# One 512-column matmul in place of two 256-column ones in the four output projections

## The chip, the cores and the metric

The kernel runs on one core of one Trainium2 chip. The metric is the device time of one execution in microseconds (us). Single matmuls are told in nanoseconds (ns).

## What is computed

Two small networks follow each other on one sequence of 256 tokens with a model width of 2048, all in 32-bit floats. Cut to what the change touches:

```
# first block: state-space mixer, then sparse attention, each with a residual and a layer norm
proj = x @ w_in;  yg = gated, scan-mixed rows of width 4096
h = yg @ ssd_w_out                      # 4096 -> 2048   (o1)
x = layer_norm(ALPHA * x + h)
o = attention rows of width 4096, gated
h = o @ dsa_w_out                       # 4096 -> 2048   (o2)
x = layer_norm(ALPHA * x + h)
# second block: gated MLP, then stick-breaking attention, each with a residual
y = u * mixed * silu(zg)                # width 4096
h = h + y @ a_w_out_2                   # 4096 -> 2048   (o3)
o = attention rows of width 2048, gated
h = h + o @ b_w_out_2                   # 2048 -> 2048   (o4)
return rms_norm(h, final_g)
```

## The kernel before

Every weight matrix is streamed once from memory. A unit is one stretch of 1024 columns' worth of weights: SyncE fetches it in 512 KB into one of four `RAW` buffers, ScalarE rounds it to a high part (`wh`, line 1074), VectorE forms the low part (`wl`, line 1502), both in the TensorE type float32r, and TensorE multiplies three times: activations high by weights high, high by low, low by high. `Plan` sets the order of the units and the buffers into which they go, and TensorE, ScalarE, VectorE and SyncE all walk that order; small tasks of other steps (transposes, attention products) run between two units.

In most projections the weights are the stationary operand and 256 tokens are the moving one, so that a matmul has 256 columns. In the projections that are in `TOKENS` it is the other way round: 128 tokens of the activation tile `X` are stationary and the weights move. Those are the four output projections `o1` to `o4`, and `cq`, `v5` and `v7`. The three last stream up to 512 columns of weights in one matmul; the output projections stream 256 at a time (line 750).

An output projection is cut into five blocks of columns, `LAST_COLS`: three of 512 columns and two of 256. For each 128 rows of the contraction there are two token halves `t` and three products, and in a block of 512 columns each of these is two matmuls, at columns 0 and 256, with the same stationary tile, which is loaded anew for each. A 512-column unit has two such 128-row tiles: 2 x 2 x 3 x 2 = 24 matmuls. A 256-column unit has four tiles and 24 matmuls also. A block of 512 float columns fills one PSUM bank of `G` for each token half.

Where a buffer starts within 512 bytes is set by hand: `STILL` is byte 128 and `MOVING` is byte 496. The activations of the output projections, `YY`, start at `STILL`. Their weights lie in the buffers `W0m`, `W1m` and `W2m` and, for some units, in spare buffers `WA`, `WB` and `WC`; all these start at `MOVING`. Most other projections use `W0` to `W2`, `WY` and `W7`, at `STILL`, with the activations `AA` and `CQ` at `MOVING`. `cq` and the first units of `v5` and `v7` have `AA` stationary; from there on `v5` and `v7` use a copy of it in the upper half of `YY`, which the profile names `YY`. All tiles are multiples of 512 bytes apart from these starts. The profile prints one line number, 672, for all matmuls, since a helper `mm` issues them; 685 is the helper for transposes.

Of the kernel before, what the change touches and what calls it, by code (L numbers as in the profile page):

```python
# [194 lines left out]
def program(nc, A, out, at, bank, counting):  # L195
# [38 lines left out]
    def on(*event):  # L234
        if counting:
            return unit_done.sem, 1
        name, n = at[event]
        return signals[name].sem, n
# [428 lines left out]
    def tensor_program():  # L667
# [3 lines left out]
        def mm(o, l, r, start, stop):  # L671
            return e.matmul(o, l, r, start=start, stop=stop, skip_group_check=True)  # L672
# [16 lines left out]
        def unit(u, part=None):  # L689
            b, kts, width, _ = units[u]  # L690
            name, i = b
# [44 lines left out]
            for j, k in enumerate(kts):  # L736
                if u == 0 and j == 1:
                    e.wait_ge(*on("rest", 0))
                if name == "bc" and i == 0 and k % 2 == 0:
                    e.wait_ge(*on("xt", k))  # L740
                if name in ("q", "qi") and i == 0 and k == 0:
                    e.wait_ge(*on("cq"))
                if name in ("o1", "o2", "o3", "o4") and i < 2 and k % 4 == 0:
                    e.wait_ge(*on(name + "_in", k // 4))
                if b in (("cq", 0), ("v5", 0)) and k % 4 == 0:
                    e.wait_ge(*on("at1" if name == "cq" else "at2", k // 4, 1 if part is None else part))
                if b == ("q7", 0) and P * k in [c for c, _ in LAST_COLS]:
                    e.wait_ge(*on("at3", k))
                if name in TOKENS:
                    step = 256 if name in ("o1", "o2", "o3", "o4") else 512  # L750
                    cols = range(0, width, step)
                    for t in range(2) if part is None else (part,):
                        xh, xl = (X[:, k, q, t * P:(t + 1) * P] for q in range(2))
                        for x, w in ((xh, wh), (xh, wl), (xl, wh)):
                            for c in cols:
                                last = mm(G[:, half + t, c:c + min(step, width)], x, w[:, j, c:c + min(step, width)],
                                          k == 0 and c == 0 and x is xh and w is wh, k == nk - 1 and x is xl)
                else:
                    for f in range(width // P):
                        o = G[:, half + f // 2, (f % 2) * T:(f % 2 + 1) * T]  # L760
                        h, l = wh[:, j, f * P:(f + 1) * P], wl[:, j, f * P:(f + 1) * P]
                        mm(o, h, X[:, k, 0, :], k == 0 and f % 2 == 0, False)
                        mm(o, h, X[:, k, 1, :], False, False)
                        last = mm(o, l, X[:, k, 0, :], False, k == nk - 1)
# [266 lines left out]
        def set8():  # L1031
            here(unit_done, "end7", "unit")
            here(pe_made, "end7", "pe")
            yield

        walk(unit, dict(turn_in=turn_in, dt_task=dt_task, ssd=ssd, gate_z=gate_z, ln_close=ln_close,
                        set3=set3, ev_cq=ev_cq, ev_ms=ev_ms, index=index, attend=attend,
                        set4=set4, ev_u5=ev_u5, set6=set6, ev_o3=ev_o3, scale7=scale7,
# [1353 lines left out]
```

## Time and profile before

| what | value |
|---|---|
| median of three runs | 2424.24 us (2424.21 to 2425.11) |
| span of the profiled execution | 2422.2 us |
| what lies outside the span (median less span) | 2.0 us |
| TensorE busy in the span | 2412.6 us of 2422.2, 19584 matmuls |
| VectorE, ScalarE busy | 1571.3 us (65%), 1243.8 us (51%) |
| weights and data moved | 467.90 MB, mean 193 GB/s |

The duration of one matmul in the profile (275 ns for 256 columns) holds its way through the array, which overlaps with the next one. What a stream of matmuls costs is read from their starts: the start of the group behind less the start of the group, divided by the count.

### The profile page before, as it was taken

Reading aid. Unit: us, or ns where it says so; the run is one execution under the profiler, and the core shown is the slowest. Engines: PE = TensorE matmul, PEld = TensorE weight load, DVE = VectorE, ACT = ScalarE, POOL = GpSimd, SP = SyncE. Lnnn points to the kernel's source line nnn. Section 1 sums busy time; section 2 is a strip of 40 time slices with the busy share of each in tenths; the row PEclk is TensorE's granted clock in tenths of the full one; section 3 lists DMA queues with packets and bytes.
Section 4 is the critical chain, followed back from the end, with each engine's and each line's share of the span. In section 5 each row is a group of like instructions: output and inputs, shape, how many; then the busy total and the mean of one; then the engine's idle time right before and its main releaser. Section 6 shows DMA issues by size and latency. Waiting matters only on the chain.

```text
span 2422.2 us, 45365 instructions
## 1 busy us (share of the span) xinstructions
PE 2412.6 (100%) x19584; PEld 2336.7 (96%) x19584; DVE 1571.3 (65%) x2104; ACT 1243.8 (51%) x1427; POOL 88.8 (4%) x68
## 2 busy tenths in 40 slices
PE   9999999999999999999999999999999999999998
PEld 9999999999999999999988899999999999999998
DVE  6778888865577766665575556656655555555556
ACT  5446665654364565554464445445444445455463
POOL 0001000100031000000000000000000000000002
PEclk9999999999999999999999999999999999999999
DMA  8666666657755655547657666666655576655645
GB/s 258 197 194 185 207 189 186 187 182 246 235 164 165 192 166 149 161 152 243 222 193 240 196 198 194 194 185 196 182 188 190 188 239 204 184 173 173 192 157 183
DMA packets 265048, 467.90 MB, mean 193 GB/s; under 512 B 18512, under 2 KB 68240, under 8 KB 262928
## 3 DMA queue, kind: packets, MB, share of 16 engines
q1 hardware_dynamic: 264704, 464.74, 61.9%
q8 instruction: 154, 2.52, 0.4%
q14 instruction: 46, 0.38, 0.0%
q10 hardware_dynamic: 144, 0.26, 0.0%
HBM read 452.16 MB, written 4.26 MB: 188 GB/s over the span
## 4 chain that ended last, share of the span: by engine, by line
PE 98%; DVE 1%; DMA 1%; ACT 0%; issue 0%; ACTq 0%
PE G L672 91%; PE M L672 5%; PE M L685 1%; DMA RAW<-in_ssd_w_in 1%; DVE W2m L1502 0%; DVE W0m L1502 0%; DVE E L1585 0%; ACT W0m L1074 0%; DVE E L1626 0%; DVE SZ L1656 0%; DVE E L1587 0%; DVE W L1498 0%; ACT L1154 0%; DVE W L1502 0%; DVE W1m L1502 0%
## 5 line engine op out<-in xcount | busy, mean ns | idle before, releaser
L672 PE MATMUL G<-AA,W 128*128 128x256 f32 x7908 | 936.7, 277 | 0.6 <-DVE AA L1506 0.4
L672 PEld LDWEIGHTS G<-AA,W 128*128 128x128 f32 x7908 | 914.7, 188 | 5.6 <-issue 3.5
L1502 DVE TENSOR_TENSOR W<-RAW,W 128x1024 fp32r<-128x1024 f32 (+1 forms) x445 | 556.0, 1252 | 361.1 <-ACT W L1074 359.9
L1074 ACT CAST W<-RAW 128x1024 fp32r<-128x1024 f32 (+1 forms) x445 | 463.7, 1047 | 457.1 <-PE G L672 447.7
L672 PE MATMUL G<-AA,WY 128*128 128x256 f32 x2508 | 304.2, 277 | 0.0
L672 PEld LDWEIGHTS G<-AA,WY 128*128 128x128 f32 x2508 | 293.0, 188 | 1.7 <-issue 1.2
L1502 DVE TENSOR_TENSOR WY<-RAW,WY 128x1024 fp32r<-128x1024 f32 (+1 forms) x112 | 140.9, 1260 | 73.8 <-ACT WY L1074 73.8
L672 PE MATMUL G<-W0m,YY 128*128 128x256 f32 x1512 | 183.7, 276 | 0.4 <-DVE W0m L1502 0.2
L672 PE MATMUL G<-W1m,YY 128*128 128x256 f32 x1512 | 183.1, 276 | 0.1
L672 PE MATMUL G<-W,YY 128*128 128x512 f32 x792 | 181.3, 389 | 0.0
L672 PE MATMUL G<-W2m,YY 128*128 128x256 f32 x1488 | 180.4, 276 | 0.0
L672 PEld LDWEIGHTS G<-W,YY 128*128 128x128 f32 x792 | 148.4, 188 | 30.7
L672 PEld LDWEIGHTS G<-W0m,YY 128*128 128x128 f32 x1512 | 176.9, 188 | 1.0 <-DVE W0m L1502 0.8
L672 PEld LDWEIGHTS G<-W1m,YY 128*128 128x128 f32 x1512 | 176.6, 188 | 0.8 <-DVE W1m L1502 0.6
L672 PEld LDWEIGHTS G<-W2m,YY 128*128 128x128 f32 x1488 | 174.0, 188 | 0.2
L1074 ACT CAST WY<-RAW 128x1024 fp32r<-128x1024 f32 (+1 forms) x112 | 116.2, 1043 | 100.2 <-PE G L672 98.6
L1502 DVE TENSOR_TENSOR W1m<-RAW,W1m 128x1024 fp32r<-128x1024 f32 x63 | 78.5, 1246 | 77.0 <-ACT W1m L1074 76.9
L1502 DVE TENSOR_TENSOR W2m<-RAW,W2m 128x1024 fp32r<-128x1024 f32 x62 | 76.9, 1240 | 68.9 <-ACT W2m L1074 68.6
L1502 DVE TENSOR_TENSOR W0m<-RAW,W0m 128x1024 fp32r<-128x1024 f32 x63 | 78.2, 1241 | 65.3 <-ACT W0m L1074 65.1
L1074 ACT CAST W1m<-RAW 128x1024 fp32r<-128x1024 f32 x63 | 66.2, 1050 | 82.6 <-PE G L672 78.7
L1074 ACT CAST W0m<-RAW 128x1024 fp32r<-128x1024 f32 x63 | 66.2, 1051 | 80.9 <-PE G L672 80.8
L1074 ACT CAST W2m<-RAW 128x1024 fp32r<-128x1024 f32 x62 | 65.2, 1052 | 80.2 <-PE G L672 78.5
(301 smaller groups left out, 2387.4 us busy)
## 6 DMA issues: line engine op xcount, KB each, us to landing
RAW<-in_a_w_in SPq DMA_DIRECT2D x192, 512.0 KB, 4.0
RAW<-in_ssd_w_in SPq DMA_DIRECT2D x160, 512.0 KB, 4.4
RAW<-in_b_w_in SPq DMA_DIRECT2D x128, 512.0 KB, 4.0
RAW<-in_dsa_w_in SPq DMA_DIRECT2D x72, 512.0 KB, 3.6
RAW<-in_ssd_w_out SPq DMA_DIRECT2D x64, 512.0 KB, 4.8
RAW<-in_dsa_w_out SPq DMA_DIRECT2D x64, 512.0 KB, 4.1
RAW<-in_a_w_out SPq DMA_DIRECT2D x64, 512.0 KB, 3.7
RAW<-in_b_w_out SPq DMA_DIRECT2D x32, 512.0 KB, 3.7
```

What stands on the lines that cost most here:

```text
L672: return e.matmul(o, l, r, start=start, stop=stop, skip_group_check=True)
L685: return e.transpose(o, i, idn)
L1074: e.copy(wh[:, 0:n], RAW[:, v % NR, 0:n]).then_inc(*up(cast_done, "cast", v))
L1502: e.tensor_tensor(wl[:, 0:n], RAW[:, v % NR, 0:n], wh[:, 0:n].bitcast(F), ALU.subtract).then_inc(*up(rest_done, "rest", v))
```

## The change

In the projections of `TOKENS` the step over the weight columns becomes 512 for all, so that `o1` to `o4` stream a 512-column tile in one matmul. Blocks of 256 columns keep one matmul of 256 for each product. Buffers and their addresses, the order of the units, the products and their order within a tile, the signals and everything on the other engines stay.

```
                 if name in TOKENS:
-                    step = 256 if name in ("o1", "o2", "o3", "o4") else 512
+                    step = 512
                     cols = range(0, width, step)
```

TensorE's instructions at the start of `o1`, among the last tasks of the state-space mixer, before:

```order
L672 MATMUL G<-W0m,YY 128x256 x24
L685 MATMUL M<-ident,XG 128x128 x4
L672 MATMUL G<-W2m,YY 128x256 x24
L685 MATMUL M<-ident,XG 128x128 x4
L672 MATMUL G<-W1m,YY 128x256 x24
```

and now:

```order
L672 MATMUL G<-W0m,YY 128x512 x12
L685 MATMUL M<-ident,XG 128x128 x4
L672 MATMUL G<-W2m,YY 128x512 x12
L685 MATMUL M<-ident,XG 128x128 x4
L672 MATMUL G<-W1m,YY 128x512 x12
```

Nothing moved: 24 matmuls of a unit became 12 of twice the width, and the transposes stand between the same units.

TensorE's instructions near the end of `o4`, where the last 512-column block ends and the first of 256 columns begins, before:

```order
L672 MATMUL G<-W0m,YY 128x256 x24
L672 MATMUL G<-W2m,YY 128x256 x24
L672 MATMUL G<-W1m,YY 128x256 x24
L672 MATMUL G<-W0m,YY 128x256 x24
L672 MATMUL G<-W2m,YY 128x256 x24
```

and now:

```order
L672 MATMUL G<-W0m,YY 128x512 x12
L672 MATMUL G<-W2m,YY 128x512 x12
L672 MATMUL G<-W1m,YY 128x256 x24
L672 MATMUL G<-W0m,YY 128x256 x24
L672 MATMUL G<-W2m,YY 128x256 x24
```

The last three rows, units of a 256-column block, are the same in both.

## Rows read from the trace of the kernel before

**Rows 1.** The page's head: busy us (share of span) x instructions; then clock by slice.

```profile
span 2422.2 us, 45365 instructions
PE 2412.6 (100%) x19584; PEld 2336.7 (96%) x19584; DVE 1571.3 (65%) x2104; ACT 1243.8 (51%) x1427; POOL 88.8 (4%) x68
...
PEclk9999999999999999999999999999999999999999
```

**Rows 2.** The page's chain that ended last, by engine and by line.

```profile
PE 98%; DVE 1%; DMA 1%; ACT 0%; issue 0%; ACTq 0%
PE G L672 91%; PE M L672 5%; PE M L685 1%; DMA RAW<-in_ssd_w_in 1%; DVE W2m L1502 0%; DVE W0m L1502 0%; DVE E L1585 0%; ACT W0m L1074 0%; DVE E L1626 0%; DVE SZ L1656 0%; DVE E L1587 0%; DVE W L1498 0%; ACT L1154 0%; DVE W L1502 0%; DVE W1m
```

**Rows 3.** Waits of TensorE: waiting line, releaser, us in total, times, longest.

```profile
PE M L672 <- POOL ident L2265: 1.6, 1, 1.6
PE G L672 <- DVE AA L1506: 0.4, 2, 0.3
PE G L672 <- DVE W0m L1502: 0.2, 1, 0.2
PE G L672 <- DVE W L1502: 0.2, 1, 0.2
```

**Rows 4.** Groups by line and shape: count, busy us, mean ns, idle before.

```profile
L672 PE MATMUL G<-W0m,YY 128*128 128x256 f32 x1512 | 183.7, 276 | 0.4 <-DVE W0m L1502 0.2
L672 PE MATMUL G<-W1m,YY 128*128 128x256 f32 x1512 | 183.1, 276 | 0.1
L672 PE MATMUL G<-W2m,YY 128*128 128x256 f32 x1488 | 180.4, 276 | 0.0
...
L672 PE MATMUL G<-WB,YY 128*128 128x256 f32 x408 | 47.7, 275 | 0.0
L672 PE MATMUL G<-WA,YY 128*128 128x256 f32 x408 | 47.6, 275 | 0.0
...
L672 PE MATMUL G<-WC,YY 128*128 128x256 f32 x48 | 5.9, 275 | 0.0
```

**Rows 5.** Timeline (start us, length us) of TensorE inside o1.

```profile
640.77 2.88 PE L672 MATMUL G<-W1m,YY 128*128 128x256 f32 x24
643.49 2.88 PE L672 MATMUL G<-W0m,YY 128*128 128x256 f32 x24
646.21 13.76 PE L672 MATMUL G<-WA,YY 128*128 128x256 f32 x120
659.81 1.52 PE L672 MATMUL G<-W2m,YY 128*128 128x256 f32 x12
```

**Rows 6.** Timeline of TensorE: v5 from the copy in YY, then u5.

```profile
1296.29 109.00 PE L672 MATMUL G<-W,YY 128*128 128x512 f32 x480
1405.13 8.36 PE L672 MATMUL G<-AA,W 128*128 128x256 f32 x72
```

**Rows 7.** Timeline of TensorE: cq, with AA stationary.

```profile
685.39 8.56 PE L672 MATMUL G<-W,AA 128*128 128x512 f32 x36
693.79 2.94 PE L672 MATMUL G<-WA,AA 128*128 128x512 f32 x12
696.57 0.64 PE L672 MATMUL G<-AA,W 128*128 128x256 f32 x4
```

**Rows 8.** Timeline of TensorE: 384-column products of the stick-breaking attention.

```profile
2031.00 0.33 PE L672 MATMUL M<-SPH,TGR 128*128 128x384 f32 x1
2031.17 0.34 PE L672 MATMUL M<-SPL,TGR 128*128 128x384 f32 x1
```

**Rows 9.** Page's groups: weight loads, us busy, mean ns, idle before.

```profile
L672 PEld LDWEIGHTS G<-W,YY 128*128 128x128 f32 x792 | 148.4, 188 | 30.7
L672 PEld LDWEIGHTS G<-W0m,YY 128*128 128x128 f32 x1512 | 176.9, 188 | 1.0 <-DVE W0m L1502 0.8
```

**Rows 10.** Timeline of TensorE: a unit right behind transposes, o3 and v5.

```profile
1815.79 1.04 PE L685 MATMUL M<-ident,RES 128*128 128x128 f32 x8
1816.58 3.04 PE L672 MATMUL G<-W2m,YY 128*128 128x256 f32 x24
1819.46 2.88 PE L672 MATMUL G<-W1m,YY 128*128 128x256 f32 x24
...
1226.97 3.04 PE L672 MATMUL G<-WB,AA 128*128 128x512 f32 x12
1229.85 0.60 PE L685 MATMUL M<-ident,XH 128*128 128x128 f32 x4
```

**Rows 11.** Busy us by engine in stretches of o1, o3; then clock, DMA share, GB/s.

```profile
575.00:620.00 45.00, 45.00 (x399) 45.00 (x399) 28.47 (x28) 20.42 (x20) 0.00 (x0) 1.00 0.78 254
...
1820.00:1860.00 40.00, 40.00 (x355) 40.00 (x354) 21.07 (x22) 16.35 (x18) 0.00 (x0) 1.00 0.57 193
```

## The prediction, made before the changed kernel ran

> **What bounds the kernel now.** I read the head of the page first: the reader is to see that TensorE is busy for 2412.6 of 2422.2 us and that its granted clock stands in the top tenth in all 40 slices [rows 1]. The chain that ended last confirms it: 98% TensorE, 91% of it products into G [rows 2]. Last the waits: in the whole execution TensorE waits for other engines 2.4 us, and 0.2 us of it is in an output projection [rows 3]. So the time is the sum of the distances between the starts of 19584 matmuls, and the question is whether two starts of 256 columns take longer than one of 512. What the other engines do counts only if TensorE gets ahead of them.
>
> **How many matmuls the change touches.** The three 512-column blocks of an output projection take 2 token halves x 3 products x 3 blocks x 2 column halves = 36 matmuls for each 128 rows of the contraction. There are 32 + 32 + 32 + 16 = 112 such row tiles in the four projections, so 4032 matmuls of 256 columns become 2016 of 512, and 2016 weight loads fall away with them. The two 256-column blocks have 2 x 3 x 2 x 112 = 1344, which stay. Together 5376, and the groups with YY stationary and 256 columns hold 1512 + 1512 + 1488 + 408 + 408 + 48 = 5376 [rows 4]. In us: 4032 at the rate read below are 457 us, 19% of the span, and 1 ns on each merged matmul is 2.0 us.
>
> **The rate now.** In o1, 120 matmuls from WA start at 646.21 and the next group at 659.81: 13.60 us / 120 = 113.33 ns each. The units on both sides have 24 in 2.72 us, the same 113.3 [rows 5]. Two of them, which is what one new matmul replaces, take 226.67 ns. At 2.4 GHz, the upper of the clock's two levels and the one granted there (1.00) [rows 11], 256 columns are 106.67 ns and 512 are 213.33, so there is an overhead of 6.67 ns on a matmul of 256. The whole question is whether this overhead belongs to the matmul or to its columns.
>
> **The rate then, from the nearest rows.** The kernel has 512-column matmuls with the stationary tile in the same buffer YY, at the same start within 512 bytes: v5, once it reads its copy. 480 of them run from 1296.29 to 1405.13: 108.84 us / 480 = 226.75 ns [rows 6]. That is twice 113.33 within 0.1 ns: the overhead went with the columns. What differs from the changed kernel is one thing, the start of the moving weights: byte 128 there, byte 496 in W0m, W1m, W2m, WA, WB and WC. In cq, where AA at byte 496 is stationary, the start of the moving weights can be compared: 36 matmuls from W (byte 128) take 8.40 us, 233.3 ns each, and 12 from WA (byte 496) take 2.78 us, 231.7 ns each [rows 7]. The start of the moving side makes little difference there, and the stationary side's makes 6.6 ns (233.3 against 226.75). Stationary at 128 and moving at 496 with 512 columns does not occur in the trace. I take 226.75, the row with the same stationary buffer and more than an order of magnitude more matmuls. The steady part is 2016 x (226.75 - 226.67) = +0.2 us. The bounds on both sides: above, the 233.3 of cq, 2016 x 6.67 = +13.4 us; below, the bare 213.33 ns of the columns, 2016 x 13.33 = -26.9 us, which no stream of this type in the trace reaches.
>
> **Breaks.** At 18 places in the 512-column blocks tasks of other steps stand between two units. The unit behind such a break takes longer: in o3 2.88 us from start to start against 2.72, so +0.16 [rows 10]. The 512-column unit behind transposes in v5 also takes 2.88, which is +0.16 over twelve at 226.67 and +0.08 over twelve at its own 233.3 [rows 10]. So each break costs the same as now or 0.08 less: 0 to -1.4 us, and I take -0.4, nearer to none, since the stationary side of that row is the other one. The signal of a unit comes with its last matmul, which starts 113 ns earlier than now and is 114 ns longer (389 mean against 275), so that VectorE and ScalarE see each unit end at the same time as before.
>
> **Other work.** Nothing is added elsewhere. VectorE and ScalarE are busy for 28.47 and 20.42 of 45 us in a stretch of o1, 21.07 and 16.35 of 40 in o3, and the DMA queues 0.78 and 0.57 [rows 11]: if the units became 3% shorter (2.64 us), these would stand at some 65%, 47% and 0.80, and still deliver. This cover is needed only in the faster case. At the start of o1 VectorE is late once already, by 0.2 us [rows 3]; a faster unit would wait there, at most some tenths of a us.
>
> **Sum.** Against the profiled execution: 2422.2 + 0.2 - 0.4 = 2422.0 us span; with the 2.0 us that lie outside, 2424.0 us. A measurement of this kernel tells about 0.2%, 4.8 us, from no change, which is 2.4 ns on each merged matmul.
>
> **Rival 1: the overhead is one for each matmul, faster.** For: every matmul loads its stationary tile, the loader's groups in the 256-column stream are busy nearly without idle (176.9 us busy, 1.0 idle), and with 512 columns it has 30.7 us of idle on 148.4 busy [rows 9], so the 256-column rate could be the loader's. Then 512 at byte 496 would pay the 6.67 ns once: 220.0 ns, 2016 x 6.67 = -13.4 us, 2410.6. The one row with a moving side at byte 496 and a stationary side at 128 that is wider than 256 is the 384-column product: 170 ns from start to start [rows 8]. In proportion to columns it would be 170.0 and with one overhead 166.67; the row is read to 10 ns only and decides nothing by itself. A path between, the 170 and 128 bare columns (53.3), gives 223.3 ns, -6.8 us, 2417.2. Against: 226.75 in v5 [rows 6], where a matmul also has one load and pays 13.4 ns. The rival must hold that byte 128 on the moving side costs that second 6.7 ns.
>
> The Trainium skill has a rule of this kind ("TensorE: Matmul & The Clock Gate", Back-to-back issue gap): N / 2.4 + 2.5 ns for each matmul when the clock is up, a fixed part that a merged matmul pays once. By it the change would give 2016 x 2.5 = 5.0 us, 2419. This trace does not agree: the rule has 109.2 and 215.8 ns where the rows have 113.33 and 226.75 [rows 5, 6]. The same section has sustained streams at other rates, which no row here shows either.
>
> **Rival 2: the long stream at byte 496 does not fall into step with the loads, slower.** The rate of 512-column matmuls depends on where operands start: 226.75, 231.7, 233.3 [rows 6, 7]. The 256-column stream at 128/496 has the good rate, and so has the 512-column one at 128/128; nothing says that 512 at 128/496 has it. If each merged matmul behaves as those of cq do, the place is every unit of the 512-column blocks and the price is 2016 x (231.7 - 226.67) = +10.1 us to 2016 x 6.67 = +13.4 us: 2434.1 to 2437.5. It decides against me from 2.4 ns on each. Against: in cq the slow rate stays whichever start the moving side has, so it goes with the stationary side.
>
> **Rival 3: nothing of it happens.** The instruction order of the changed kernel shows twelve 128x512 where there were twenty-four 128x256, in all 512-column blocks, so this is excluded.
>
> **How the numbers follow.** Forecast (in proportion to columns, 2422.6 to 2425.5): 0.42. Rival 1 in its two sizes, 2410.6 to 2417.2, and the rule of the Trainium skill beside it: 0.30. Rival 2, 2434 to 2437.5: 0.28. Faster by over 0.2% (under 2419.4) takes rival 1, 0.31; slower by over 0.2% (over 2429.1) takes rival 2, 0.28; within, 0.41. Both signs hold more than the forecast, so its own range stands apart: 2422.6 to 2425.5. The range for 8 in 10 reaches over both rivals: 2409.5 to 2438.0. It leaves out a rate under 219.5 ns and one over 233.5.
>
> **What would show it.** In the changed kernel the timeline of o1 between 575 and 626 us is a stream without breaks: a unit of twelve takes 2.72 us if I am right, 2.64 for the single overhead, 2.78 to 2.80 for rival 2. v5's 480 matmuls must still take 108.84 us, and the 256-column blocks 2.72 a unit. TensorE's waits must stay at 2.4 us. If the units take 2.72 and the time still differs, the cause is the breaks or the waits. I would be wrong first in the step that takes v5's rate for a moving side that starts elsewhere.

## The result and the profile after

| | median | runs |
|---|---|---|
| before | 2424.23 us (2423.46 to 2426.29) | 8 |
| changed | 2430.66 us (2430.08 to 2431.54) | 8 |

The ratio is 1.0027, with a 95% interval of 1.0018 to 1.0036: the change makes the kernel slower by 0.27%, 6.4 us. The forecast was no change at 2424.0; the time lies inside the wide range and outside the forecast's own.

The head of the page after, with the same columns as [rows 1]:

```profile
span 2429.7 us, 41333 instructions
...
PE 2419.7 (100%) x17568; PEld 2255.5 (93%) x17568; DVE 1571.8 (65%) x2104; ACT 1243.3 (51%) x1427; POOL 88.4 (4%) x68
...
PEclk9999999999999999999999999999999999999999
```

19584 - 2016 = 17568 matmuls, as foretold; 2016 weight loads are gone; VectorE and ScalarE work as before; the clock is at its upper level throughout. TensorE is busy 7.1 us longer all the same. The timeline of TensorE (start us, length us) in o1 shows where:

```profile
609.77 2.93 PE L672 MATMUL G<-W0m,YY 128*128 128x512 f32 x12
612.55 8.48 PE L672 MATMUL G<-WA,YY 128*128 128x512 f32 x36
620.87 2.94 PE L672 MATMUL G<-W2m,YY 128*128 128x512 f32 x12
623.64 2.94 PE L672 MATMUL G<-W1m,YY 128*128 128x512 f32 x12
```

A unit of twelve takes 2.77 us from start to start, and 36 matmuls take 8.32: 231.1 ns each, where two of 256 columns took 226.67 [rows 5]. The 480 matmuls of v5 still take 226.75 and the 256-column blocks 113.3, so only the merged ones changed. The single starts in the trace, which the timeline merges, show more: 225, 231, 237 or 238 ns, over and over. Three of them are 693.3, 231.1 on the mean. Before, single starts were 113 or 114 ns apart without any such cycle.

The rate is not the same everywhere. This is o4 in the same execution, around the last task with 128-column products:

```profile
2345.72 2.93 PE L672 MATMUL G<-W2m,YY 128*128 128x512 f32 x12
2348.49 2.93 PE L672 MATMUL G<-W1m,YY 128*128 128x512 f32 x12
...
2352.36 2.94 PE L672 MATMUL G<-W0m,YY 128*128 128x512 f32 x12
2355.14 2.88 PE L672 MATMUL G<-W2m,YY 128*128 128x512 f32 x12
2357.86 2.88 PE L672 MATMUL G<-W1m,YY 128*128 128x512 f32 x12
2360.58 1.47 PE L672 MATMUL M<-LSB,V 128*128 128x256 f32 x8
```

Ahead of the task a unit takes 2.77 us, behind it 2.72, from the same buffers. At the start of o1 two short pieces run at 226.7 as well, 48 matmuls from 499.85 and 12 from 513.21, each begun behind a wait.

TensorE's waits after (columns as in [rows 3]):

```profile
PE M L672 <- POOL ident L2265: 1.6, 1, 1.6
PE G L672 <- DVE W1m L1502: 0.7, 1, 0.7
PE G L672 <- DVE AA L1506: 0.4, 1, 0.4
PE G L672 <- DVE W0m L1502: 0.4, 2, 0.3
```

VectorE is 1.1 us late at the start of o1, against 0.2.

**Where the 7.5 us between the two spans lie**, taken between points of equal work in the two traces (the end of a wide block is set 18 matmuls into the 256-column block behind it, so that its settling is counted in): up to o1 -0.7; the first 13 us of o1, with its waits, +0.7; the rest of o1's wide blocks +2.0; o2's +2.2; o3's +2.5; o4's +0.8; everything else -0.1. The head of the kernel, which the change does not touch, took between 0.7 less and 0.1 more than before in the seven kernels below that leave it as it is, so it shifts by some tenths on its own. In a steady stretch of o1, 225 merged matmuls (51.0 us before) take 1.00 us more, 4.4 ns each; o3's 576 take 2.49, 4.3 each.

### The profile page after: what moved, and what is told of

It is laid out like the page before. It is cut to its first block, busy times and chain, and to the rows that moved or that the text cites. A ratio compares the mean times of both kernels' runs of the same rounds, so it can differ in the third digit from the quotient of the medians.

```text
span 2429.7 us, 41333 instructions
## 1 busy us (share of the span) xinstructions
PE 2419.7 (100%) x17568; PEld 2255.5 (93%) x17568; DVE 1571.8 (65%) x2104; ACT 1243.3 (51%) x1427; POOL 88.4 (4%) x68
## 4 chain that ended last, share of the span: by engine, by line
PE 95%; DVE 2%; ACT 1%; DMA 1%; issue 1%; POOL 0%; SPq 0%; ACTq 0%; POOLq 0%
PE G L672 89%; PE M L672 5%; PE M L685 1%; DMA CSB<-cs_scratch 1%; DVE W L1502 0%; ACT W L1074 0%; DVE E L1626 0%; POOL YT L2282 0%; DVE WY L1502 0%; DVE E L1585 0%; DVE XG L1524 0%; DVE E L1587 0%; DVE YT L1640 0%; DVE XG L1531 0%; DVE W1m L1502 0%
## 5 line engine op out<-in xcount | busy, mean ns | idle before, releaser
L672 PE MATMUL G<-W1m,YY 128*128 128x512 f32 (+1 forms) x900 | 185.5, 356 | 0.7 <-DVE W1m L1502 0.7
L672 PE MATMUL G<-W0m,YY 128*128 128x512 f32 (+1 forms) x888 | 185.8, 359 | 0.4 <-DVE W0m L1502 0.4
L672 PE MATMUL G<-W2m,YY 128*128 128x512 f32 (+1 forms) x876 | 182.7, 358 | 0.0
L672 PEld LDWEIGHTS G<-W1m,YY 128*128 128x128 f32 x900 | 148.3, 188 | 27.4 <-DVE W1m L1502 1.3
L672 PEld LDWEIGHTS G<-W0m,YY 128*128 128x128 f32 x888 | 147.5, 188 | 27.7 <-DVE W0m L1502 1.4
L672 PEld LDWEIGHTS G<-W2m,YY 128*128 128x128 f32 x876 | 145.4, 188 | 26.5 <-DVE W2m L1502 0.2
```

## The experiments

Two theories stood at the outset. **A**: where the moving tile starts within 512 bytes decides, together with the width, at what rate a stream settles, and 496 is bad for 512 columns. **B**: the width and the work beside the output projections decide, and the start does not.

**512 columns with the weights at byte 128**, against the changed kernel.

```
-            w = (W3M if units[u][0][0] in ("o1", "o2", "o3", "o4") else W3)[s]
+            w = W3[s]
...
-            o += (MOVING - o) % 512      # in spare(): WA, WB, WC
+            o += (STILL - o) % 512
```

> The changed kernel (512 columns) with the output projections' weights in buffers that start at byte 128 within 512 in place of 496. Theory A (the start of the moving side sets the rate of a 512-column stream): units of twelve take 2.72 us as in v5 (226.7 ns each) and not 2.77 (231.1), so 2016 x 4.4 ns = 8.9 us less than the changed kernel; about 2424 us, as before the change. Theory B (the rate comes from the width and from what runs beside the output projections, the start does not matter): units stay at 2.77 us, time near 2430.7. The spare buffers WA and WB also serve cq and v5 on AA, 120 matmuls, where the start moved the rate by 1.6 ns at most, 0.2 us.

Measured: 2432.3 us, ratio to the kernel before 1.0033 (1.0020 to 1.0045). The total fits B; the timeline does not:

```profile
611.17 8.32 PE L672 MATMUL G<-WA,YY 128*128 128x512 f32 x36
619.33 8.32 PE L672 MATMUL G<-W,YY 128*128 128x512 f32 x36
627.49 11.68 PE L672 MATMUL G<-WA,YY 128*128 128x256 f32 x96
639.00 6.16 PE L672 MATMUL G<-W,YY 128*128 128x256 f32 x50
```

36 of 512 columns take 8.16 us: 226.7 ns, as A has it; between points of equal work the wide blocks take what they took before, within 0.1 us each, beyond the first 13 us of o1 (+1.0). But the 256-column blocks, whose buffers had moved too, take 11.51 us / 96 = 119.9 ns and not 113.3. There are 1344 of these, 9.0 us by count and 8.6 found, and they give back what the wide ones had gained. The expectation had counted one width alone.

**256 columns with the weights at byte 128**, the same edit on the kernel before.

> The kernel before (256 columns in the output projections) with their weights at byte 128. Theory A in its wide form (start and width together decide, and 496 is there for the 256-column stream): 256 columns at 128 are slower than 113.3 ns, with 118 to 120 ns as right behind a break; 5376 matmuls x 5 to 6.7 ns = +27 to +36 us, 2451 to 2460. Theory B: 113.3 ns whatever the start, no change, 2424.2.

Measured: 2457.23 us, ratio 1.0136 (1.0121 to 1.0151), 32.9 us more than the kernel before, measured beside it (2424.38).

```profile
616.51 8.80 PE L672 MATMUL G<-WA,YY 128*128 128x256 f32 x72
625.15 8.80 PE L672 MATMUL G<-W,YY 128*128 128x256 f32 x72
```

8.64 us / 72 = 120.0 ns. B falls: width and neighbours are as before, the start alone turns 113.3 into 120.0. 5376 x 6.67 = 35.8 is about the loss, less the pieces behind breaks that had 118 to 120 before too.

**v5 and v7 with their weights at byte 496**, against the kernel before.

```
-            w = (W3M if units[u][0][0] in ("o1", "o2", "o3", "o4") else W3)[s]
+            w = (W3M if units[u][0][0] in ("o1", "o2", "o3", "o4", "v5", "v7") else W3)[s]
```

> The kernel before, with the weights of v5 and v7 at byte 496 in W0m to W2m in place of 128 (x7's buffer W7 stays). The output projections are as before. Theory A: the 512-column matmuls of v5 and v7 on the copy in YY go from 226.75 to 231.1 ns; 792 matmuls in W buffers, +3.5 us. Theory B: they stay at 226.75.

Measured: 2427.16 us in one run against 2424.38. The stream that the prediction had taken as its nearest row [rows 6], now:

```profile
1310.23 2.93 PE L672 MATMUL G<-W1m,YY 128*128 128x512 f32 x12
1313.00 2.94 PE L672 MATMUL G<-W0m,YY 128*128 128x512 f32 x12
```

2.77 us for twelve: the start alone turns 226.7 into 231.1, in another projection, with the output projections untouched. Between points of equal work the stretch with v5 takes 1.9 us more than before and the one with v7 1.4, 3.2 of the 3.5 expected. Theory A holds both ways.

**A scan of streams alone.** Nothing else runs in this kernel; after four fp32 matmuls each stream begins anew. Its core:

```
for n, so, mo in CASES:                      # columns, start of stationary, start of moving side
    for u in range(8): for j in range(2): for t in range(2):
        for x, w in ((xh, wh), (xh, wl), (xl, wh)):
            for col in range(0, 512, n):
                mm(G[:, t, col:col + n], x, w[:, col:col + n], ...)
    warm(4)
```

> Not the network: 38 streams of 96 (512 columns) or 192 (256) products of the same three-product pattern as in an output projection, one after another behind four fp32 matmuls each, with nothing beside them, over starts of the stationary and the moving side within 512 bytes and over widths. The output is only the input copied. Theory A: with the stationary side at 128, 512 columns take 231.1 ns with the moving side at 496 and 226.7 at 128; 256 take 113.3 at 496; and other starts fall on these or further levels. Theory B: with no other engine at work 512 at 496 takes 226.7 too, and all starts of the moving side are alike. 496/128 and 496/496 should show the 231 to 233 of cq.

The first streams in its timeline are 512 columns at 128/496 (stationary/moving), 512 at 128/128, then 256 at 128/496 and 256 at 128/128:

```profile
23.38 22.43 PE L42 MATMUL G<-W,X 128*128 128x512 f32 x96
45.65 1.05 PE L42 MATMUL M<-ident 128*128 128x128 f32 x8
46.46 22.06 PE L42 MATMUL G<-W,X 128*128 128x512 f32 x96
68.36 1.06 PE L42 MATMUL M<-ident 128*128 128x128 f32 x8
...
115.74 22.07 PE L42 MATMUL G<-W,X 128*128 128x256 f32 x192
137.65 1.05 PE L42 MATMUL M<-ident 128*128 128x128 f32 x8
138.46 23.28 PE L42 MATMUL G<-W,X 128*128 128x256 f32 x192
161.57 1.05 PE L42 MATMUL M<-ident 128*128 128x128 f32 x8
```

From start to start the four take 22.27, 21.90, 21.91 and 23.11 us, the settling included. The distances of starts in the second half of each stream give the settled rate:

| stationary/moving | 512 columns, ns | 256 columns, ns |
|---|---|---|
| 128/496 | 231.1 | 113.3 |
| 128/128 | 226.7 | 120.0 |
| 496/128 | 233.3 | 120.0 |
| 496/496 | 233.3 | 118.3 |
| 0/0, 256/256 | 226.7, 226.6 | 120.0, not run |
| 0/256 | 226.7 | 120.0 |
| 0/368 | not run | 113.3 |

So the loss needs no other engine and no DMA. The scan also shows why cq misled: with the stationary side at 496 both starts of the moving side give 233.3, while at 128 they differ by 4.4.

**A finer scan**: stationary at 128, the moving side at every 16th byte for 512 columns and every 8th for 256.

> Not the network: streams of the three-product pattern alone, stationary side at byte 128, moving side at every 16th byte for 512 columns (72 matmuls each) and every 8th for 256 (144 each). The output is only the input copied. Theory A: each width has its own set of good starts, 512 at 128 and 384 (226.7) and 256 near 496 (113.3), and others lie 2 to 10 ns above per 512 columns. Open: whether any start is under 226.7 or 113.3; if the overhead could be had once for each matmul, some start shows 220 for 512.

Settled at 226.7 with 512 columns: 112, 128, 368 and 384. Settled at 113.3 with 256 columns: 64, 192, 240, 320, 448 and 496. All others lie between 228.8 and 234.7, or 116.6 and 122.5; the values repeat with a period of 256 bytes, within 0.1 ns but for one pair (512 columns at 0 and 256, 1.1 apart). No start of the moving side is good for both widths, and none is under 226.66 or 113.32. The 220 ns of rival 1 does not appear. Not every value repeats at the same addresses: 512 columns at 128/112 ran at 226.7 here and at 236.7 in the first scan, 256 columns at 128/256 at 118.7 here and at 120.0 there, and 512 columns at 128/0 and 128/256 differ by 1.0 between the scans.

**Other products, and another lead.** The rows of the changed kernel at 226.7 and the value at 112 ask whether a stream has one rate at all.

```
made = {"same": ((xh, wh),) * 3, "xonly": ..., "wonly": ...,
        "turned": ((xh, wh), (xl, wh), (xh, wl))}.get(mode, ((xh, wh), (xh, wl), (xl, wh)))
...
if mode[:4] == "lead":                       # two short matmuls of k columns ahead of the stream
    mm(M[:, 0:k], X[:, so:so + P], W[:, mo:mo + k], True, True)   # twice
```

> Not the network: streams at fixed starts with another pattern of products: all three alike (one stationary, one moving tile), only the stationary tile changing, only the moving one, and the second and third product exchanged; then 32 streams of 512 columns at 128/496, each behind two short matmuls of 16 to 512 columns. The output is only the input copied. Theory A1 (the repeating 225, 231, 237 ns is the three products, each with its own distance between tiles): with all products alike a single value stays, with the order exchanged the sequence changes, and what stands ahead does not matter. Theory A2 (it is the phase between two readers that settles into one of two states, 226.7 or 231.1): the lead decides for some of the 32 streams, which run at 226.7 from the start to the end at the same addresses, as three stretches of the changed kernel did.

A1 falls. With all products alike, 512 columns at 128/496 still run 225, 231, 237; the cycle of three has nothing to do with the three products. At 128/128 and 128/384 all five patterns settle at 226.7, and at 256 columns all keep 113.3 (496) and 120.0 (128). At 128/240 four patterns run at 231.1 to 231.3, and the one with all products alike runs at 226.7 from its second matmul on. Whether the products or what stood ahead made that difference, the scan does not tell. A2 stands: of 32 leads at 128/496, those of 64 and 128 columns make the stream run at 226.66 from its second matmul to its last, the other thirty at 230.9 to 231.3. The lead of 64 and its neighbour of 80:

```profile
766.86 0.39 PE L50 MATMUL M<-W,X 128*128 128x64 f32 x2
767.08 16.58 PE L50 MATMUL G<-W,X 128*128 128x512 f32 x72
783.50 1.05 PE L50 MATMUL M<-ident 128*128 128x128 f32 x8
784.31 0.39 PE L50 MATMUL M<-W,X 128*128 128x80 f32 x2
784.53 16.88 PE L50 MATMUL G<-W,X 128*128 128x512 f32 x72
801.25 1.05 PE L50 MATMUL M<-ident 128*128 128x128 f32 x8
```

16.42 against 16.72 us for the same 72 matmuls on the same tiles.

**The start chosen by width**, against the changed kernel.

```
-            w = (W3M if units[u][0][0] in ("o1", "o2", "o3", "o4") else W3)[s]
+            w = (W3M if units[u][0][0] in ("o1", "o2", "o3", "o4") and units[u][2] < 512 else W3)[s]
```

> The changed kernel with the start of W0 to W2 chosen by width in the output projections: byte 128 for units of 512 columns, byte 496 for units of 256 (WA, WB, WC stay at 496). Theory A (each width has its own good start, nothing else was lost): 1848 merged matmuls go from 231.1 to 226.7 ns, -8.1 us against the changed kernel, and the 256-column blocks keep 113.3; 168 from WA and WB stay at 231.1, +0.7 us. So 2423 to 2425, equal to the kernel before. Rival (a part of the loss comes from breaks or waits that 512 columns bring): 1 us or more stays over the kernel before, beyond the 0.7.

Measured: 2424.78 us against 2423.80 of the kernel before, measured beside it, ratio 1.0003 (0.9994 to 1.0013), no difference that the measurement can tell. Between points of equal work, with the 18 matmuls behind, o3's wide blocks take 134.48 us (134.49 before, 136.99 changed). The stretches with WA and WB, still at 496, are 0.5 us longer each, 1.0 and not 0.7, since a stream that changes between the two starts settles anew each time:

```profile
603.32 8.37 PE L672 MATMUL G<-W,YY 128*128 128x512 f32 x36
611.53 8.47 PE L672 MATMUL G<-WA,YY 128*128 128x512 f32 x36
619.84 8.37 PE L672 MATMUL G<-W,YY 128*128 128x512 f32 x36
```

8.21 us for 36 from W right behind WA (228.1 each), 8.31 for WA. TensorE's waits here are near the changed kernel's, 1.4 us for W at line 1502 where that had 1.1 for W1m and W0m. The first 13 us of o1 take 1.1 us more than before and the head of the kernel 0.7 less, where the changed kernel had 0.7 and 0.7: most of the one is given back by the other.

**o3 alone at 512 columns**, against the kernel before.

```
-                    step = 256 if name in ("o1", "o2", "o3", "o4") else 512
+                    step = 256 if name in ("o1", "o2", "o4") else 512
```

> The kernel before with 512-column matmuls in o3 alone, starts as before. Theory A: 576 merged matmuls x 4.4 ns = 2.6 us in the stretch of o3's three wide blocks (134.5 us before), everything else as before; single run at about 2426.8. Rival (some of the loss is at the start of o1, where VectorE is late): the rest of the changed kernel's loss lies outside these 2.6 x 3.5 = 9.0 us.

Measured: 2426.26 us in one run against 2423.80, +2.5. o3's wide blocks take 136.99 us, +2.49, the very value of the changed kernel, and every stretch behind o1's start and outside o3 is within 0.03 us of before. TensorE waits 0.9 us for the low parts in W1m and W0m at line 1502, in the o1 that is as before:

```profile
PE G L672 <- DVE W1m L1502: 0.6, 1, 0.6
...
PE G L672 <- DVE W0m L1502: 0.3, 1, 0.3
```

So the wait there, 0.2 in one execution of the kernel before, is up to 0.9 without the change; the 1.1 of the changed kernel cannot be put down to it.

**Two short matmuls ahead of each stretch, in the network**, against the changed kernel. `broken` is set again by every other task and by every unit of another projection.

```
+                            if name[0] == "o" and width == 512 and broken[0]:
+                                for _ in range(2):
+                                    mm(G[:, half + t, 0:64], x, w[:, j, 0:64], k == 0, False)
+                                broken[0] = False
```

> The changed kernel (512 columns at byte 496) with two more matmuls of 64 columns ahead of the first unit of an output projection's 512-column stretch that follows anything else (21 places, 42 short matmuls, 2.4 us of columns and loads at most if each costs 57 ns). They use the tiles of the product behind them and add to its sums, so those sums are not the reference's. Theory A2 (two states of one stream, picked by the phase at its start; 64 columns picked the fast one behind transposes when alone): most stretches run at 226.7 ns from start to end, 8 us less in them, plus the cost of the short ones: 2423.5 to 2426. Rival (the state depends on what runs beside it in the network and is lost again): 231.1 stays, 2431 to 2433.

Measured: 2433.8 us, ratio to the kernel before 1.0040 (1.0026 to 1.0055), above both ranges. As a forecast A2 missed, in the time and in "most stretches"; that there are two rates and that the lead changes which one comes is seen again. Of 21 stretches, four ran at 226.7 as a whole: two of 12 matmuls, one of 36 (in o4, which had it in the changed kernel too) and the longest, 432 matmuls of o2, which had 231.3 on the mean in the changed kernel and has 226.9 here:

```profile
1087.85 3.19 PE L673 MATMUL G<-W0m,YY 128*128 128x64 f32 x14
1090.89 2.88 PE L673 MATMUL G<-W2m,YY 128*128 128x512 f32 x12
1093.61 2.88 PE L673 MATMUL G<-W1m,YY 128*128 128x512 f32 x12
```

It lasts until the 256-column block at 1186.09, through 98 us of casts and transfers beside it. But a rate does not always last until the next break. In a stretch of 36 in o2 the first two units run at 231 and the third at 226.7, with no wait between them that the profile shows:

```profile
1062.64 2.93 PE L673 MATMUL G<-W1m,YY 128*128 128x512 f32 x12
1065.40 2.89 PE L673 MATMUL G<-W0m,YY 128*128 128x512 f32 x12
```

In the changed kernel TensorE starts this unit from W0m 0.1 us late. The remaining stretches stay at 231; what ends ahead of them differs, which may be why and was not tested one by one. Each pair costs some 0.2 us (0.23 from its start at 1821.68 to the first wide one at 1821.91), so that 21 pairs cost more than the 2 us that some 470 matmuls gain.

**The same with 128 columns.** Only the width of the short ones differs.

> As the kernel with the two short matmuls of 64 columns, but of 128 columns, the other width that picked the fast state when alone, and the width of the products ahead of one stretch of o4 that ran at 226.7 in the changed kernel. Theory A2: the same stretches as with 64, or others where the streams ahead end otherwise; single run 2424 to 2427. Rival: 2431 to 2434.

Measured: 2433.33 us in one run, in the range of the rival and not in that of A2. Now o2's long stretch is back at 231.2 and o4's stretch of 36 at 231. Two short stretches of o1 (12 and 24 matmuls) run at 226.7, and so do the first 24 of the 36 in o2 shown above, whose last twelve run at 231: the switch at the same unit, the other way round. And a stretch of o3 runs at the lower value, 192 matmuls between two groups of transposes at 227.0 on the mean, where the changed kernel has 231.6. This kernel, then the changed one, at that place:

```profile
1823.16 3.19 PE L673 MATMUL G<-W2m,YY 128*128 128x128 f32 x14
1826.19 2.88 PE L673 MATMUL G<-W1m,YY 128*128 128x512 f32 x12
1828.91 2.88 PE L673 MATMUL G<-W0m,YY 128*128 128x512 f32 x12
```

```profile
1821.69 3.02 PE L672 MATMUL G<-W2m,YY 128*128 128x512 f32 x12
1824.55 2.94 PE L672 MATMUL G<-W1m,YY 128*128 128x512 f32 x12
1827.33 2.94 PE L672 MATMUL G<-W0m,YY 128*128 128x512 f32 x12
```

2.72 against 2.78. Which stretch gets which value changes with its lead, and both occur on the same addresses in the same network. With one lead for all, no kernel here ran at the lower value everywhere.

## Why the prediction was right and wrong

**What bounds the kernel, and how many matmuls are touched:** right. TensorE is busy for the whole span after as before, 2016 matmuls and loads fell away, and the loss is the distance of starts times that number.

**The rate now:** right, 226.67 ns for two [rows 5].

**The rate then:** this step failed, in the sentence that took 226.75 from v5 [rows 6] for a moving side that starts elsewhere. The prediction named this as the place where it would be wrong first. The size: 4.4 ns on each merged matmul, 8.9 us by count, where the term was +0.2; 7.3 us are found up to the last merged matmul of each projection, the first 13 us of o1 left out. The rate itself was right for byte 128; what was missing was a row with 512 columns at 128/496. The argument that closed the gap compared two starts of the moving side in cq [rows 7], with the stationary side at 496. The scan shows that this comparison holds for that side only. A difference that is absent under one setting of the other operand says nothing about the other setting. And the 231.7 was read from one unit of twelve. The trace of before has another from the same kind of buffer on AA,

```profile
682.52 3.04 PE L672 MATMUL G<-WA,AA 128*128 128x512 f32 x12
```

whose single starts are 233 and 234 ns apart once it has settled, while those of the unit at 693.79 are 230 to 232. The first unit of cq, at 671.99, has 228 and 232 in turn, and in the changed kernel, with the same buffers, 233 and 234. So that a 512-column stream has more than one rate at the same starts stood in these rows already.

**The overhead goes with the columns:** right as a number at good starts (113.3 and 226.7), and wrong as a rule. At one start, byte 128, 256 columns cost 13.3 ns over their bare time and 512 cost 13.3 as well; at byte 496 it is 6.7 and 17.8.

**Rival 1, an overhead for each matmul:** it had 0.30 and fell. No start in the finer scan is under 226.66 for 512 columns. The 170 ns of [rows 8] spoke for neither: a stream of 384 columns alone settles at 173.3 at both starts. The 2.5 ns of the Trainium skill ("TensorE: Matmul & The Clock Gate", Back-to-back issue gap), which that section gives for an isolated matmul, would by an estimate have given a gain of 5 us. The trace shows a loss.

**Rival 2, the long stream at byte 496 does not fall into step:** the slower rate is what happened, with 0.28; that it comes from falling out of step with the loads is not shown. Its price was too high: it went by the 231.7 to 233.3 of cq, +10.1 to +13.4 us, 2434.1 to 2437.5, and the stream has 231.1. At 231.1 the sum would have been +8.9, less 0.4 for the breaks, 2432.7 against 2430.66. The measured time lies between the forecast's own range and that of this rival, in neither.

**The breaks:** the term was -0.4 in a range of 0 to -1.4, and it came out nearer the far end. In the changed kernel the unit behind the transposes in o3 takes 2.86 us (1821.69 to 1824.55) where a settled one takes 2.77, +0.09 in place of +0.16. Stretch by stretch the wide blocks take 1.6 us less than 4.4 ns on each matmul would give: 0.4 us of that is the 96 matmuls that ran at 226.7, and the rest lies at the breaks and waits, 0.05 to 0.07 at most of them. With 512 columns at the good start there is next to nothing: from o2's first matmul to the second unit behind the last of seven breaks, the kernel with the start chosen by width takes 47.45 us against 47.50 before.

**What lies outside the span:** the 2.0 us were taken from the median of three runs and one span. The profiled runs of the changed kernel and of the first experiment have 1.3 us outside their spans (2431.06 and 2429.7, 2432.56 and 2431.3), so the profiled execution of before was probably one of the shorter ones, 0.7 us under its median. That of the changed kernel was 0.4 over its own. That would be why the spans differ by 7.5 and the medians by 6.4.

**What stays open.** That two readers of one memory, the loader of the stationary tile and the stream of the moving one, meet in a repeating way fits all of this: a rate set by both starts, values that mostly repeat after 256 bytes, two states that the lead picks. It was argued and not shown; no view tells who waits inside a matmul. A longer load is not seen: in the scan's streams of 512 columns a weight load lasts 187 or 188 ns at 226.7 as at 233.3. What switches the rate inside a stretch is open too. The Trainium skill ("TensorE: Matmul & The Clock Gate", Step-by-step: what each phase is for) says that the two have independent read ports and that loading the next tile takes no read bandwidth from the running matmul. In the scan, where nothing else reads, the rate of a stream changes with the start of the stationary side alone (226.7 at 128/128, 233.3 at 496/128). So here the measurement decides that the pace of the matmuls does depend on where the loaded tile lies; in what way, it does not tell.

## What to carry to other kernels

In a kernel that is bound by a stream of matmuls, the width of the moving side and the start addresses of both sides are one choice: change one and measure again the other, for every width that shares the buffers. A good rate in another stage is a price for this one only if width, stationary start and moving start all agree. Before an edit to the network, a kernel of bare streams over starts and widths gives these rates in one run of 0.9 to 1.7 ms. Give each stream more than one lead, since one lead shows one state only.

## What the runs showed of the hardware

- The settled distance between float32r matmuls with a load ahead of each depends on both starts: 226.7 to 236.7 ns for 512 columns, 113.3 to 122.5 for 256, with nothing else at work. On all 5376 matmuls of the output projections, the start alone is worth 33 us, 1.4% of the kernel.
- At 128/496 with 512 columns a stream has two states, 226.7 ns, and 225, 231, 237 in turn. What runs ahead of it changes which one comes. It held over 432 matmuls in one case and switched between two units of one stretch in two others.
- In the network, settling behind a break takes the same time at both widths within 0.1 us over seven breaks when each has its good start. With 512 columns at 128/496 it takes 0.05 to 0.07 us less at most breaks.
